# Mixer projections as three fp32r products, most weight units split on GpSimd, norms reordered

## The reference

```python
x = x + rmsnorm(attention_mixer(rmsnorm(x), ...))      # A: w_in 1024x3072; chunked + stick-breaking attention
x = x + rmsnorm(swiglu(rmsnorm(x), ...))               # F0, width 2816
x = x + rmsnorm(recurrent_mixer(rmsnorm(x), ...))      # R: w_in 1024x2048, causal conv, gates, scan
x = x + rmsnorm(swiglu(rmsnorm(x), ...))               # F1
h = h + dilated_diff_mixer(rms_norm(h), ...)           # E: w_in 1024x3072; q/k norms, 16 heads
h = h + swiglu_2(rms_norm(h), ...)                     # F2
h = h + hgrn2_mixer(rms_norm(h), ...)                  # G: w_in 1024x4096; gates in logs, chunked recurrence
h = h + moe_swiglu(rms_norm(h), ...)                   # M: 8 experts of width 3584, top 2
```

## Time and profile before

| what | value |
| --- | --- |
| median of 3 runs | 2214.52 us (2212.74 to 2216.56) |
| profiled execution | 2214.71 us, span 2212.6 us |
| mean granted clock of TensorE | 0.989 of full speed |
| busy in the span | TensorE 2152.9, VectorE 1412.0, ScalarE 1182.0, GpSimd 42.6 us |
| stages (start of span at 0) | A to 168, F0 to 365, R to 464, F1 to 655, E to 818, F2 to 1007, G to 1183, then router and experts |

### The profile page before, as it was taken

How to read it: one execution, slowest core, us unless ns; L and a number is a source line. 1 busy time by engine, 2 the same in 40 slices (tenths; PEclk the granted TensorE clock), 3 DMA queues, 4 the chain that set the end, 5 groups by cost and what they waited for, 6 DMA issues and landing times.

```text
span 2212.6 us, 26593 instructions
## 1 busy us (share of the span) xinstructions
PE 2152.9 (97%) x10426; PEld 1755.4 (79%) x10426; DVE 1412.0 (64%) x1193; ACT 1182.0 (53%) x1107; POOL 42.6 (2%) x94
## 2 busy tenths in 40 slices
PE   7999999999999999999996999999999999999998
PEld 7757889868888658889874888888888888888887
DVE  1425444454444635443725888889888988888887
ACT  1335432444423544333533677677766777767775
POOL 1001000010000000000000000000000000000000
PEclk9999999999999999999996999999999999999999
DMA  7325554555554226555423999999999999999997
GB/s 250 115 77 187 191 184 149 183 174 189 189 172 143 96 86 209 184 178 162 134 77 115 359 354 351 376 341 363 348 358 349 362 348 356 372 338 373 342 362 262
DMA packets 208180, 539.60 MB, mean 244 GB/s; under 512 B 10046, under 2 KB 67487, under 8 KB 208111
## 3 DMA queue, kind: packets, MB, share of 16 engines
q1 hardware_dynamic: 204224, 530.61, 67.7%
q0 software_dynamic: 2096, 7.87, 1.0%
q10 hardware_dynamic: 1790, 0.14, 0.1%
HBM read 537.54 MB, written 1.05 MB: 243 GB/s over the span
## 4 chain that ended last, share of the span: by engine, by line
PE 89%; ACT 5%; DVE 2%; issue 2%; DMA 1%; POOL 1%; DVEq 0%; ACTq 0%; POOLq 0%
PE ps L1962 12%; PE ps L1964 12%; PE ps L1963 12%; PE ps L509 12%; PE ps L622 5%; PE ps L623 5%; PE ps L624 5%; PE ps L586 4%; PE ps L527 4%; ACT ring_r L1953 3%; PE ps L663 3%; PE ps L665 3%; PE ps L664 3%; PE ps L1972 2%; PE ps L2017 1%
## 5 line engine op out<-in xcount | busy, mean ns | idle before, releaser
L1958 DVE TENSOR_TENSOR ring_r<-ring,ring_r 128x2048 fp32r<-128x2048 f32 x339 | 761.9, 2287 | 114.8 <-ACT ring_r L1953 114.7
L1953 ACT ACTIVATE ring_r<-ring 128x2048 fp32r<-128x2048 f32 x339 | 631.0, 1911 | 70.1 <-DMA ring<-in_moe_w_gate 60.1
L1962 PE MATMUL ps<-ring_r,arena_r 128*128 128x512 f32 x1344 | 532.0, 396 | 1.0 <-DVE arena_r L2200 1.0
L1964 PE MATMUL ps<-ring_r,arena_r 128*128 128x512 f32 x1344 | 524.6, 390 | 0.0
L1963 PE MATMUL ps<-ring_r,arena_r 128*128 128x512 f32 x1344 | 524.4, 390 | 0.0
L324 DVE TENSOR_TENSOR ring_r<-ring,ring_r 128x2048 fp32r<-128x2048 f32 x99 | 226.9, 2292 | 233.2 <-ACT ring_r L315 233.2
L1964 PEld LDWEIGHTS ps<-ring_r,arena_r 128*128 128x128 f32 x1344 | 252.7, 188 | 54.7
L1962 PEld LDWEIGHTS ps<-ring_r,arena_r 128*128 128x128 f32 x1344 | 253.0, 188 | 51.6 <-issue 1.2
L1963 PEld LDWEIGHTS ps<-ring_r,arena_r 128*128 128x128 f32 x1344 | 253.3, 188 | 50.5
L315 ACT ACTIVATE ring_r<-ring 128x2048 fp32r<-128x2048 f32 x99 | 189.3, 1915 | 181.3 <-DMA ring<-in_ffn_w_up 81.6
L509 PE MATMUL ps<-arena,ring 128*128 128x128 f32 (+1 forms) x1600 | 261.7, 324 | 3.6 <-ACT arena L368 2.7
(11 more groups left out here) (322 smaller groups left out, 1798.4 us busy)
## 6 DMA issues: line engine op xcount, KB each, us to landing
ring<-in_moe_w_gate SPq DMA_DIRECT2D x115, 1024.0 KB, 5.3
ring<-in_moe_w_up SPq DMA_DIRECT2D x112, 1024.0 KB, 5.3
ring<-in_moe_w_down SPq DMA_DIRECT2D x112, 1024.0 KB, 5.0
ring<-in_ffn_w_gate SPq DMA_DIRECT2D x33, 1024.0 KB, 5.1
ring<-in_ffn_w_up SPq DMA_DIRECT2D x33, 1024.0 KB, 5.1
ring<-in_ffn_w_down SPq DMA_DIRECT2D x33, 1024.0 KB, 4.9
ring<-in_attn_w_in SPq DMA_DIRECT2D x24, 1024.0 KB, 5.3
ring<-in_hgrn_w_in SPq DMA_DIRECT2D x16, 1024.0 KB, 5.4
```

The lines of the kernel that those rows point to most:

```text
L1953: nc.scalar.activation(unit_parts(k)[0], ring[:, slot_of(k), 0:2048], ACT.Copy).then_inc(m_hi, 1)
L1958: nc.vector.tensor_tensor(low, ring[:, slot_of(k), 0:2048], high, ALU.subtract).then_inc(m_lo, 1)
L1962: nc.tensor.matmul(out_, x[:, 0, f, :], w[0], start=first, stop=False)
L1964: return nc.tensor.matmul(out_, x[:, 0, f, :], w[1], start=False, stop=last)
```

## The change

Mixer units become split units too. The first four of each mixer are split by ScalarE and VectorE as the feed-forward's are, at places in the norm; from the fifth on (`plan[4:]`) GpSimd does both, in quarters of 512 columns. Normalised tokens are always kept as high and low parts. TensorE may start on the first half (four of eight row blocks) of the tokens once that has been subtracted. One order of the norm (`norm_scalar`, `norm_vector`) serves all stages. At its end each feed-forward splits the next stage's first unit. Norm 0's gain row is loaded from ScalarE's queue as its first instruction. The experts' start splits one unit ahead of the norm, and gate values and constants come later. The scores of A and E move off page 2, which now holds the tokens' high part.

```diff
-                plan.append((kind, columns_of(w, c0, False), ...))
+                plan.append((kind, columns_of(w, c0, True), ...))
...
+        pool_units = [u for plan in (A_plan, R_plan, E_plan, G_plan) for _, u, _ in plan[4:]]
+        dve_units = [u for u in range(N1) if split_no[u] is not None and u not in pool_units]
+        low_at = {u: (w_lo, n + 1) for n, u in enumerate(dve_units)}
+        low_at.update({u: (w_lo_pool, 4 * n + 4) for n, u in enumerate(pool_units)})
...
+        def lows_gpsimd(pool, plan):
+            quarters = [slice(512 * q, 512 * q + 512) for q in range(4)]
+            for _, u, _ in plan[4:]:
+                pool.wait_ge(landed[u % NS_EARLY], landed_at(u))
+                for c in quarters:
+                    nc.gpsimd.tensor_copy(slot_hi(u)[:, c], slot_raw(u)[:, c]).then_inc(w_hi_pool, 1)
+                for q, c in enumerate(quarters):
+                    pool.wait_ge(w_hi_pool, low_at[u][1] - 3 + q)
+                    nc.gpsimd.tensor_tensor(slot_lo(u)[:, c], slot_raw(u)[:, c], slot_hi(u)[:, c],
+                                            ALU.subtract).then_inc(w_lo_pool, 1)
...
-            dve.wait_ge(gpre_in, 16 * (k + 1))
+            if k:
+                dve.wait_ge(gpre_in, 16 * k)
+            else:
+                dve.wait_ge(gpre_first_in, 16)
...
+        def norm_scalar(act, k, first):
             if has_post(k):
                 post_sums(act, k, 0)
+            if k:
+                highs_to(act, first + 1)
             norm_sums(act, k, 0)
+            highs_to(act, first)
             norm_high(act, k, 0)
             if has_post(k):
                 post_sums(act, k, 1)
+            highs_to(act, first + 2)
+            norm_sums(act, k, 1)
+            highs_to(act, first + 3)
             norm_high(act, k, 1)
 
+        def norm_vector(dve, k, first):
             if has_post(k):
                 post_gain(dve, k, 0)
+            if k:
+                residual(dve, k, 0)
+                lows_to(dve, first + 1)
             normalise_tokens(dve, k, 0)
+            lows_to(dve, first)
             norm_low(dve, k, 0)
             if has_post(k):
                 post_gain(dve, k, 1)
+            lows_to(dve, first + 1)
+            if k:
                 residual(dve, k, 1)
+            lows_to(dve, first + 2)
+            normalise_tokens(dve, k, 1)
+            lows_to(dve, first + 3)
             norm_low(dve, k, 1)
...
+        def by_columns(pe, u, bank, fs=(0, 1), ts=(0, 1), second=None):
...
+                    if second and f == fs[0] and kt == KT // 2:
+                        pe.wait_ge(*second)
                     nc.tensor.matmul(o, wh[:, kt, c], HTh[:, ts, kt, :], start=(kt == 0), stop=False)
                     nc.tensor.matmul(o, wh[:, kt, c], HTl[:, ts, kt, :], start=False, stop=False)
                     mm = nc.tensor.matmul(o, wl[:, kt, c], HTh[:, ts, kt, :], start=False, stop=(kt == KT - 1))
...
         (first_tokens)
+                if n == 0:
+                    pe.wait_ge(s_htl, 4 * k + 1)
+                how(pe, u, bank, ts=(0,), second=None if n else (s_htl, 4 * k + 2))
...
         (ffn_tensor; the same for the second token half)
+            pe.wait_ge(s_htl, 4 * k + 1)
+            gate_tokens(0, 0, 0)
             pe.wait_ge(s_htl, 4 * k + 2)
-            gate_tokens(0, 0, 0), gate_tokens(0, 1, 0)
+            gate_tokens(0, 1, 0)
...
         (ffn_scalar, at its end; lows_to in ffn_vector)
+            highs_to(act, down[CHUNKS_FF - 1, 0] + 1)
...
-        A_sc = [four(page(i)) for i in (7, 10, 11, 2)]
+        A_sc = [four(page(i)) for i in (7, 10, 11)] + [dist[:, :, :]]
...
         (M_scalar)
-            for k in range(AHEAD):
-                split_high(act, 0, k)
+            split_high(act, 0, 0)
             norm_sums(act, 7, 0)
+            split_high(act, 0, 1)
             norm_sums(act, 7, 1)
+            split_high(act, 0, 2)
...
         (M_vector: split_low(0, 0) first, split_low(0, 1) behind residual(7, 1), split_low(0, 2) behind
          tokens_low(1, 4); POS and select(0, 0) ahead of the gates and of ident_r, M_selT, M_y)
...
         (gpsimd)
-            pool.dma_start(gpre[:, :], row_of(*norm_gains[0])).then_inc(gpre_in, 16)
+            norm_gpsimd(pool, step, 0, 0)
...
             setup_gpsimd(pool, step)
+            lows_gpsimd(pool, A_plan)
...
                 if k == 2:
+                    lows_gpsimd(pool, R_plan)
                     distances_gpsimd(pool, step)
+                elif k == 4:
+                    lows_gpsimd(pool, E_plan)
+                elif k == 6:
+                    lows_gpsimd(pool, G_plan)
         (scalar, first)
+            act.dma_start(gpre[:, :], a[norm_gains[0][0]][norm_gains[0][1]].partition_broadcast(P)).then_inc(gpre_first_in, 16)
```

More of the change, by code:

```diff
@@ L189, in build @@
         w_lo = sem("w_lo")
+        w_lo_pool = sem("w_lo_pool")
+        w_hi_pool = sem("w_hi_pool")
         w_used = sem("w_used")
@@ L312, in highs_to @@
                 high_done[0] += 1
-                if split_no[u] is not None:
+                if u in dve_units:
                     act.wait_ge(landed[u % NS_EARLY], landed_at(u))
@@ L443, in norm_turn @@
                 mm.then_inc(s_tr, 1)
-        def norm_scalar(act, k):
-            for t in range(TT):
-                if has_post(k):
-                    post_sums(act, k, t)
-                norm_sums(act, k, t)
-                norm_high(act, k, t)
-        def norm_vector(dve, k):
-            for t in range(TT):
-                if has_post(k):
-                    post_gain(dve, k, t)
-                if k:
-                    residual(dve, k, t)
-                normalise_tokens(dve, k, t)
-                norm_low(dve, k, t)
@@ L519, in by_columns, with by_tokens @@
             return mm
[L521 to L529 removed]
+        def by_tokens(pe, u, bank, ts=(0, 1), second=None):
             wh, wl = (v.rearrange("p (k n) -> p k n", k=KT) for v in (slot_hi(u), slot_lo(u)))
@@ L533, in by_tokens @@
                 for kt in range(KT):
+                    if second and t == ts[0] and kt == KT // 2:
+                        pe.wait_ge(*second)
                     nc.tensor.matmul(o, HTh[:, t, kt, :], wh[:, kt, :], start=(kt == 0), stop=False)
@@ L1302, in R_vector @@
             lows_to(dve, R_out[3][0] + 1)
-        E_sc = [page(i)[:, 0:3 * KEYS].rearrange("p (n k) -> p n k", n=3) for i in (7, 8, 2)]
+        E_sc = [page(i)[:, c:c + 3 * KEYS].rearrange("p (n k) -> p n k", n=3) for i, c in ((7, 0), (8, 0), (9, 2 * KEYS))]
         E_pt = page(9)[:, 0:2 * KEYS].rearrange("p (n k) -> p n k", n=2)
@@ L2138, in M_vector @@
         def M_vector(dve, step):
-            for k in range(AHEAD):
-                split_low(dve, 0, k)
+            split_low(dve, 0, 0)
             for t in range(TT):
                 residual(dve, 7, t)
+                if t:
+                    split_low(dve, 0, 1)
                 normalise_tokens(dve, 7, t)
@@ L2225, in M_vector @@
             select(0, 0)
+            dve.wait_ge(m_ex, 1)
+            step.link(nc.vector.tensor_scalar(M_w[:, 0], M_w[:, 1], 1.0, None, ALU.add))
+            step.link(nc.vector.reciprocal(M_w[:, 0], M_w[:, 0]))
+            step.link(nc.vector.tensor_tensor(M_w[:, 1], M_w[:, 1], M_w[:, 0], ALU.mult))
+            for k, onehot in enumerate((OH0, OH1)):
+                ins = nc.vector.tensor_tensor(onehot, onehot, M_w[:, k].to_broadcast([P, TT, NE]), ALU.mult)
+            step.link(ins)
+            step.link(nc.vector.tensor_tensor(GATE, OH0, OH1, ALU.add))
+            nc.vector.tensor_copy(ident_r, ident[:, :])
+            nc.vector.memset(M_selT.bitcast(F32), 0.0)
+            step.link(nc.vector.memset(M_y.bitcast(F32), 0.0))
             nc.vector.memset(M_cnt[:, 1:2], 0.0).then_inc(m_yl, 1)
```

109 lines of the change are left out of this document (30 added, 79 removed).

## The result

The changed kernel took 2358.28 us in the median of four runs (2334.48, 2341.83, 2374.74 and 2381.50), against 2214.23 before: 144 us more. The two above 2370 are slow runs, so kernels are compared with the mean of the two faster ones, 2338.2: 124 us more, ratio 1.056, 95% interval 1.053 to 1.059. The profiled execution is the fastest, 2334.48, and is 119.8 us above that of before. The direction was forecast, the size was not: 28 us, range to 2270.

A forecast was written before the change was run, and what follows sets the result against it. TensorE, busy 97% of the span, was taken as the bound. Products +3.0, start and norms -3.9, G's chain undisturbed +1.2 and GpSimd holding VectorE +28 gave +28 on 2214.7: 2243 us, range 2211 to 2270.

The forecast's parts named there:

- The price of the products: TensorE's mixer products, each becoming three fp32r: narrow 0.110 us, wide 0.120; wide -43.7, narrow +46.7, together +3.0 us.
- rival of a cheaper narrow product (c): On TensorE, a narrow fp32r product costs less than its row, 0.08 us: 2204 us, chance 0.08.
- GpSimd's own time: GpSimd's splits of mixer units: 7.9 us a unit, bounds 5.4 and 12, just fast enough in G.
- rival (b): GpSimd takes 10 us or more a unit, so TensorE waits in G and A: 2260 to 2275, chance 0.15.
- Rival (a): The lock doesn't hold VectorE, or slack covers it; only small terms remain: 2209 to 2221, chance 0.18.
- Before the experts: At the experts' norm, splitting one unit first removes TensorE's 10.13 us idle time and slow transposes: -11.6 us in all.
- Norms 3 and 5: The copy of the feed-forward's second unit stands ahead of the norm sums on ScalarE: +3.8 and +4.6 us.
- the exclusion's step: VectorE's instructions with two SBUF operands wait for GpSimd, 0 to 1.3 us each: G 16, A 7, E 4, R 1.
- The upper bound of 70: Top of the range for GpSimd holding VectorE over all mixers: 80 instructions at 1.0 us, less slack.
- Rival (d): The norm waits at 3 and 5 come out longer, with a slowed clock after them: 2250, chance 0.04.
- The start: At norm 0, the first gain row moves to the head of ScalarE's queue: -1.5 us of a possible -3.5.

The follow-up runs named there:

- b1: The kernel before with only the change's experts' start (one unit split ahead of the norm, gate values and constants later): 2199.56 us.
- c3: On c2, the second unit's split moved behind the first norm sums on ScalarE and behind the normalising on VectorE: 2209.56 us.
- s1: On b1, projections still plain fp32, GpSimd does in G the changed kernel's copies and subtractions, into a page nobody reads: 2237.78 us.
- e2: The changed kernel with GpSimd's subtraction of each quarter directly behind its copy, so that it must wait for it: 2335.87 us.
- d2: The changed kernel with the fp32 bursts of d1 and the edit of e2: 2324.04 us.
- d1: The changed kernel with eight unread fp32 transposes after each of a mixer's first three units of the first token half: 2353.46 us.
- e1: The changed kernel without GpSimd's 32 splits; ScalarE copies and VectorE subtracts all mixer units: 2303.72 us.
- c2: On e1, each product by columns in the token halves is one plain fp32 product of the high parts, low parts left out: 2215.69 us.
- b2: On b1, the first gain row is loaded from ScalarE's queue as its first instruction: 2203.79 us.
- g1: On b1, mixer G alone uses three fp32r products, no GpSimd, first two units in token halves, the others whole: 2225.11 us.
- c1: On e1, eight unread fp32 transposes after each of a mixer's first three units of the first token half: 2289.40 us.

## Why the prediction was right in direction and wrong in size

**Right.** *The price of the products.* Narrow fp32r 0.110: measured 0.112 (144 from 1097.76 to 1113.87, G). Wide 0.120: measured 0.121 (48 from 1141.52 to 1147.32). The rival of a cheaper narrow product (c) is out. *GpSimd's own time*: 7.9 us a unit was taken, 7.2 measured where VectorE leaves it alone. In G a unit took 7.7 to 10.5 us, above the 8 at which the prediction let TensorE wait for it; TensorE did not, since it stood behind VectorE by then, and rival (b) is out. Rival (a), that the exclusion doesn't hold VectorE, is out too. *Before the experts*: -11.6 was forecast, b1 shows -13.7. *Norms 3 and 5*: waits of 4.07 and 4.19 us, forecast about 4; c3 shows that it is the order of that split.

**Wrong, first: the exclusion's step.** The step that failed is "0 to 1.3 us, about 0.5 on average when it stands alone and 1.0 when they follow one another", and the 28 us made from it. It took for granted that VectorE waits for one GpSimd instruction. In G that is what happened, but for more instructions than the 41 counted, and the chain had less slack than was let: 16 us were forecast there, s1 measured 37 with the lower clock that follows the waits. In A the 16 scans that made up most of the count met no GpSimd at all. In A and E one instruction waited 24 and 27 us for the end of GpSimd's whole queue. The forecast had 7 and 4 for these stages; taking the starvation away alone gave 15.8 and 10.7 in e2 (and 29 in all in d2 against d1, a difference with some clock in it). That a pause between GpSimd's instructions ends it is shown by e2 and d2, where the only edit is one that makes GpSimd wait for itself. Why the same train without pauses did not starve anything in G stays open. In the changed kernel itself TensorE's four new waits behind VectorE are 66 us, all gone in e1. Net, GpSimd's part is 34.5 us by e1 (54.6 by the median of all runs) in place of 28, less what ScalarE and VectorE then had to do in its stead and less 11.5 us that R lost in e1; in G, where it can be had clean, it is 37 in place of 16. The upper bound of 70 would have held it; the sum with 70 is 2285, and even that is short, so this step alone does not make up the miss.

**Wrong, second: a term that was missing.** The products were priced at TensorE's upper level only. Nothing in the sum stands for it. The trace of before hides it, for its narrow products are plain fp32 and leave the lower level soon after each idle time. With narrow fp32r products the lower level lasts: 33 us in A in each of the three kernels with four halves and no bursts, 60 in R in e2, 20 in E in e1. By c2 it is up to 38 us (its 88 less the 50 of the price; 26 from profile to profile), and the scatter between runs goes with it: in e1 2292 and 2304 go with mean clocks of 0.977 and 0.972, in d2 2300 and 2321 to 2328 with 0.981 and 0.967 to 0.970. Rival (d) had a slowed clock, but only behind the norm waits, and at 2250. The one hint, the start of before, 2.6 us longer than the same 96 records in the earlier trace rows, was there to be asked about and was not. What makes the level fall at one norm and not at the next stays open: it fell in R in e1 and e2 and not in the changed kernel.

**Wrong, small.** The start: -1.5 forecast; alone the early gain row gives nothing or costs (b2), as the first unit's load is later with it. E without GpSimd: the change had good cause not to put these splits on VectorE, which is then the bound (189.5 in e1, 170.3 in c2 against 155.8).

**The books.** From 2213.7 to 2338.2: GpSimd 34.5, lower clock 38, narrow against plain products 50, the first the difference to e1, the other two the parts of another (c2's 88; the 50 by the measured price). That leaves 2 us for the rest (c2 against before): the experts' start has -14 in it, the norm order +6 and the wide products, by their measured price, some -42 (an estimate); the 52 us that make up the sum are then the splits on VectorE and what else the norms lost. By stage c2 is 0.9 us under before in A, 10.0 over it in R, 14.5 over it in E and 19.7 under it in G, 16.1 of these from the experts' start (b1). How the 52 divide was not tried; VectorE has these splits only in e1 and c2, so the 34.5 are what GpSimd costs more than that, not what it costs against splits that are free. The differences were taken in one order only, and the parts overlap, as d1 shows.

## What to carry to other kernels

Moving work to an idle GpSimd is not free for a busy VectorE: a train of GpSimd's SBUF instructions with no pause can hold a single VectorE instruction for its whole length, whatever its size, so make GpSimd wait for its own result now and then, and look for what stands behind VectorE. Before plain fp32 products are split in three, count the narrow ones: at 128 columns three cost half as much again as one, and after idle time they may keep TensorE at its lower clock. Of a change in parts, run each part alone: here the experts' start was the only part run alone on the kernel before that paid. The wide products alone, with the narrow ones left as they were, were never run; c2 comes nearest, and at 2215.69 it is 16 us over b1.

## What the hardware showed that was not expected

- VectorE shut out by GpSimd for 24.33 and 27.28 us (the changed kernel) and for 24.23 and 27.09 (d1), each time until GpSimd's queue ended, though in G no instruction of either waited for more than about one of the other. Which of the two happens is not settled; a pause on GpSimd's side ended it in both kernels where it was tried.
- A TENSOR_SCALAR of VectorE with one SBUF operand waits for GpSimd too (0.4 to 1.15 us in s1), and one of 8 columns was starved.
- The lower clock level outlasted 60 us in which TensorE was busy 10.00 of 10.00 us. At A's start the level is seen only in the spacing of the records, 0.213 and 0.111 us: the clock column reads 1.00.
- Narrow fp32r products that began at the upper level stayed there in some places (G in the changed kernel, 92 in 10 us from 1100 on) and lost it within 3 us in others: in e1 at 385.1 and 702.6, in e2 at 388.9, in g1 at 1010.7. At the same norm 2 plain fp32 products kept it (c2).
- The level rose behind other work than theirs: fp32 transposes (45.07 in the changed kernel, 24.75 in c1, 402.39 in e1) or products of 256 columns (450.52 in e2, 1048.90 in g1). Not every burst of transposes did it: those at 384.92 in c1 and 407.94 in e2 did not.
